# Gate projections of a conformer/attention/MoE layer: seven block products for eight, weight sums made by accumulating loads, the convolution's norm moved into attention slots

## What is computed

```python
proj = x @ w_in[l] + b_in[l]                       # 1024 -> 4608 columns
glu_in, q, k, v, gate_logits = jnp.split(proj, splits, axis=-1)
y_conv = conv_branch(glu_in, ...)                  # a * sigmoid(gate) -> causal depthwise conv, 31 taps
                                                   # -> LayerNorm over 512 channels -> silu -> @ w_conv_out
y_attn = chunked_attention(heads(q), heads(k), heads(v), rel_bias[l]) @ w_attn_out[l]
g_conv, g_attn = jnp.split(jax.nn.sigmoid(gate_logits), 2, axis=-1)     # 2 x 1024 columns
mixed = (g_conv * y_conv + g_attn * y_attn) @ w_o[l] + b_o[l]
x = layer_norm(ALPHA * x + mixed, ln1_g[l], ln1_b[l])
x = layer_norm(ALPHA * x + grouped_moe(x, w_router, b_router, w_gate_up[l], w_down[l]), ln2_g[l], ln2_b[l])
```

## Time and profile before

| what | value |
|---|---|
| median of 3 runs | 1135.43 us (1131.72 to 1138.6) |
| span of the profiled execution | 1130.7 us |
| PE busy | 1098.3 us, 97% |
| DVE busy | 803.2 us, 71% |
| ACT busy | 529.2 us, 47% |
| POOL busy | 227.4 us, 20% |
| chain that ended last | PE 85%, DVE 4%, DMA 4%, ACT 3% |

### The profile page before, as it was taken

How to read it: one execution, slowest core, us unless ns; L and a number is a source line. 1 busy time by engine, 2 the same in 40 slices (tenths; PEclk the granted TensorE clock), 3 DMA queues, 4 the chain that set the end, 5 groups by cost and what they waited for, 6 DMA issues and landing times.

```text
span 1130.7 us, 17012 instructions
## 1 busy us (share of the span) xinstructions
PE 1098.3 (97%) x5583; PEld 913.1 (81%) x5584; DVE 803.2 (71%) x1152; ACT 529.2 (47%) x787; POOL 227.4 (20%) x190
## 2 busy tenths in 40 slices
PE   8999999999999999999999999999999999999984
PEld 7888888888978789878888888787888888888762
DVE  5799999935447766666685588888679556558866
ACT  5111111123456665645331134467578545557755
POOL 0000000000046864757100000013121211212110
PEclk9999999999999999999999999999999999999998
DMA  7121233232111010181632325889999876699966
GB/s 266 56 84 56 83 104 104 83 112 93 57 38 43 19 43 1 65 326 39 251 118 88 142 119 196 278 331 354 324 331 381 311 230 192 236 352 341 368 177 269
DMA packets 49800, 199.58 MB, mean 177 GB/s; under 512 B 7249, under 2 KB 7633, under 8 KB 47682
## 3 DMA queue, kind: packets, MB, share of 16 engines
q1 hardware_dynamic: 43538, 176.19, 41.9%
q0 software_dynamic: 6192, 22.49, 8.0%
HBM read 166.21 MB, written 32.52 MB: 176 GB/s over the span
## 4 chain that ended last, share of the span: by engine, by line
PE 85%; DVE 4%; DMA 4%; ACT 3%; POOL 2%; issue 2%; ACTq 0%; DVEq 0%; SPq 0%; POOLq 0%
PE ps L544 16%; PE ps L546 16%; PE ps L545 16%; PE ps L1570 9%; PE ps L1572 9%; PE ps L1571 9%; PE ps L644 2%; PE ps L630 2%; DMA gu<-in_wexp 2%; PE ps L616 2%; DMA dn_raw<-in_wexp 2%; PE ps L1651 1%; PE ps L1566 1%; POOL pr L499 1%; PE ps L1678 1%
## 5 line engine op out<-in xcount | busy, mean ns | idle before, releaser
L544 PE MATMUL ps<-xh,wh 128*128 128x512 f32 x512 | 203.3, 397 | 2.0 <-DVE xl L1030 1.7
L545 PE MATMUL ps<-xl,wh 128*128 128x512 f32 x512 | 199.5, 390 | 0.0
L546 PE MATMUL ps<-xh,wl 128*128 128x512 f32 x512 | 199.5, 390 | 0.0
L1469 DVE TENSOR_TENSOR gu<-gu (+1 forms) x128 | 148.6, 1220 | 33.6 <-issue 21.5
L499 POOL TENSOR_SCALAR pr<-pr,rinv 128x640 f32<-128x640 f32 (+4 forms) x64 | 95.4, 1503 | 379.7 <-DVE rinv L1153 379.5
L1052 DVE SCALAR_TENSOR_TENSOR cv<-u,dw_t,cv 128x1024 f32<-128x1024 f32 x120 | 154.1, 1284 | 3.7
L1570 PE MATMUL ps<-gu,xgh 128*128 x336 | 134.0, 399 | 4.0 <-DVE gu L1469 2.2
L1463 ACT ACTIVATE gu<-gu (+1 forms) x128 | 124.4, 1048 | 20.6 <-DMA gu<-in_wexp 13.0
L1572 PE MATMUL ps<-gu,xgl 128*128 x336 | 131.9, 393 | 0.0
L1571 PE MATMUL ps<-gu,xgh 128*128 x336 | 131.4, 391 | 0.0
L544 PEld LDWEIGHTS ps<-xh,wh 128*128 128x128 f32 x512 | 96.1, 188 | 25.4 <-issue 6.4
(11 more groups left out here) (278 smaller groups left out, 2022.4 us busy)
## 6 DMA issues: line engine op xcount, KB each, us to landing
gu<-in_wexp SPq DMA_DIRECT2D x64, 1024.0 KB, 9.1
dn_raw<-in_wexp SPq DMA_DIRECT2D x16, 2048.0 KB, 9.8
raw<-in_wblk SPq DMA_DIRECT2D x52, 512.0 KB, 4.2
gate_cols<-gst SPq DMA_DIRECT2D x16, 512.0 KB, 5.3
xf<-acc_rows SPq DMA_DIRECT2D x8, 512.5 KB, 8.1
xraw<-in_xT SPq DMA_DIRECT2D x8, 512.0 KB, 7.3
gcm<-gate_cols SPq DMA_DIRECT2D x8, 512.0 KB, 7.5
gam<-gate_cols SPq DMA_DIRECT2D x8, 512.0 KB, 14.5
```

The lines of the kernel that those rows point to most:

```text
L544: pe.matmul(o, a_h, b_h, start=first, stop=False)
L545: pe.matmul(o, a_h, b_l, start=False, stop=False)
L546: return pe.matmul(o, a_l, b_h, start=False, stop=last)
L1469: eng.tensor_tensor(gu[:, par, k, 1, :], gu[:, par, k, 1, :].bitcast(F32), gu[:, par, k, 0, :], ALU.subtract).then_inc(gu_lo, 1)
```

## The change

A pair of gate blocks (two blocks of 128 columns) against two halves of the inputs and two halves of the tokens is a two-by-two product of blocks. It took eight block products; after the change it takes seven (the Strassen-Winograd scheme), on sums of weight quarters and sums of x quarters, and seven additions of results. A block product is 4 input tiles by 3 matmuls of 512 columns, 12 matmuls. There are 8 pairs (`KC`), so 56 products (`N_UNITS`), in the order 1, 6, 5, 7, 2, 3, 4 (`ORDER`) within a pair.

- **Weights.** A "unit" (`uraw`, `uh`, `ul`, eight slots in the place of the weight ring) is a sum of one to four quarters of 256 KB. The first quarter is loaded, the others are added by DMAs that accumulate into SBUF. All of them, 15 for each pair and 120 in all, are issued by POOL, and each accumulating one waits until the one before it has landed.
- **x.** Four sums of quarters of x are made once by DVE (`input_sums`), split by ACT and DVE (`t_high`, `t_low`).
- **Results.** ACT copies product 1 out of PSUM, DVE makes seven additions of 512 columns for a pair (`gate_sums`), ACT takes the sigmoid in place, SP stores halves of 256 KB.
- **Convolution.** One tap beside each product (`TAPS_A_PRODUCT`), two beside each value tile, the last ten behind the value tiles. The mean comes between the half sums of q and k, the squares behind it, the variance in slot 1 (`VAR_SLOT`), the reciprocal in slots 2 and 3, `normalise` in slots 4 to 7, the silu in slot 9 (`SILU_SLOT`).
- The scaling of the first two biases goes from DVE to POOL. Value tiles use banks 0 to 3, so that the q/k half sums wait for all of them (`v_lo`).

Many semaphores are shared, with new counts; this part of the diff is left out.

```diff
+UNIT_SLOTS = 8
+PARTS = {1: ((0, 0),), 2: ((0, 1),), 4: ((1, 1),), 5: ((1, 0), (1, 1)), 6: ((1, 0), (1, 1), (0, 0)),
+         7: ((0, 0), (1, 0)), 3: ((1, 0), (1, 1), (0, 0), (0, 1))}
+ORDER = (1, 6, 5, 7, 2, 3, 4)
...
+                def add_piece(m, p):
+                    if 0 <= m < N_UNITS and p < len(PARTS[UNITS[m][0]]):
+                        s = m % UNIT_SLOTS
+                        pool.wait_ge(u_in[s], unit_in(m, p - 1))
+                        pool.dma_start(uraw[:, s], unit_rows(m, p), accum_op=ALU.add).then_inc(u_in[s], 16)
+                def load_unit(m):
+                    if m < UNIT_SLOTS:
+                        pool.wait_ge(blk_used, B_V[0] - RING + m // 2 + 1)
+                    elif m < N_UNITS:
+                        pool.wait_ge(blk_used, B_V[0] + m - UNIT_SLOTS + 1)
+                    if m < N_UNITS:
+                        pool.dma_start(uraw[:, m % UNIT_SLOTS], unit_rows(m, 0)).then_inc(u_in[m % UNIT_SLOTS], 16)
+                load_unit(0)
+                for m in range(N_UNITS + 2):
+                    load_unit(m + 1)
+                    add_piece(m, 1)
+                    add_piece(m - 1, 2)
+                    add_piece(m - 2, 3)
...
+                def gate_product(m):
+                    x, q = UNITS[m]
+                    s, bank = m % UNIT_SLOTS, m % 8
+                    pe.wait_ge(u_lo, m + 1)
+                    if m < 8:
+                        pe.wait_ge(u_ready, CB - 1 + (m >= 4))
+                    else:
+                        bank_read(m - 8)
...
+                    for k in range(CB):
+                        last = mm3(ps[:, bank, :], uh[:, s, k], ul[:, s, k], b_h[:, k, :], b_l[:, k, :],
+                                   k == 0, k == CB - 1)
...
-                for g in range(LAST_GATES[0]):
-                    gate_job(g)
-                conv_mean()
-                gate_job(LAST_GATES[0])
-                conv_var()
-                gate_job(LAST_GATES[1])
+                for m in range(N_UNITS):
+                    gate_product(m)
...
+                pe.wait_ge(v_lo, TT)
                 for i in range(2):
                     pe.wait_ge(w_lo, B_Q[0] + i + 1)
...
                     for h in range(2):
                         half_sum(B_Q[0] + i, h, ps[:, 2 * i + h, :], 0, KC).then_inc(qk_done, 1)
+                        if i and h == 0:
+                            conv_mean()
...
+                for m in range(N_UNITS):
+                    if m + 4 < N_UNITS:
+                        unit_low(m + 4)
+                    elif m + 4 < N_UNITS + 2:
+                        low(B_V[0] + m + 4 - N_UNITS)
+                    if m == 0:
+                        glu(CB - 1)
+                    if m:
+                        gate_sums(m - 1)
+                    some_taps(TAPS_A_PRODUCT)
+                gate_sums(N_UNITS - 1)
...
+                def conv_late(n):
+                    if n == 0:
+                        for j in range(1, CB):
+                            square_sum(j)
+                    if n in (2, 3):
+                        dve.wait_ge(sq_done, CB + 1)
+                        for i in range(2 * n - 4, 2 * n - 2):
+                            c = slice(2 * P * i, 2 * P * i + 2 * P)
+                            dve.reciprocal(rstdc[:, c], std[:, c]).then_inc(nrm, 1)
+                    if 4 <= n < 4 + CB:
+                        normalise(n - 4)
```

More of the change, by code:

```diff
@@ L899, in v_high @@
+                for m in range(N_UNITS + 2):
+                    if m < N_UNITS:
+                        copy_product(m)
+                    if m + 4 < N_UNITS:
+                        unit_high(m + 4)
+                    elif m + 4 < N_UNITS + 2:
+                        high(B_V[0] + m + 4 - N_UNITS)
+                    for q, slot in sigmoids_at(m):
+                        gate_sigmoid(q, slot)
                 def v_high(s, t, o):
@@ L952, in _ @@
                 for i in range(2):
-                    act.wait_ge(gs_out[i], 16 * KC)
+                    for slot in range(4):
+                        act.wait_ge(row_moved[4 * i + slot], GATES_STORED)
                 def conv_high(n):
@@ new lines, in _ @@
+                assert taps == CB * CW
+                for i in range(2):
+                    qk_low(i, ps[:, i, :])
+                dve.wait_ge(stat_done, 1)
+                for j in range(CB):
+                    dve.scalar_tensor_tensor(out=cv[:, j, :], in0=psf[:, 4 * HALF:6 * HALF], scalar=-1.0 / DC, in1=cv[:, j, :],
+                                             op0=ALU.mult, op1=ALU.add).then_inc(cent, 1)
+                for i in range(2, 4):
+                    qk_low(i, ps[:, i, :])
@@ L1131, in maxima @@
+                for i in range(2):
+                    for slot in range(4):
+                        dve.wait_ge(row_moved[4 * i + slot], GATES_STORED)
                 def maxima(n):
@@ L2176, in two_a_block @@
         return columns(w).reshape(KC // 2, 2, P, CB, P).transpose(0, 2, 1, 3, 4).reshape(KC // 2, P, KC, P)
[L2177 removed]
+    first, gates = block_columns()
+    w_in = columns(w_in)
+    blocks = np.concatenate([w_in[first], two_a_block(w_conv_out), two_a_block(w_attn_out), columns(w_o), w_in[gates]])
     rel = np.clip(np.arange(P)[:, None] - np.arange(BANDW)[None, :] + 512, -256, 256) + 256
```

434 lines of the change are left out of this document (270 added, 164 removed).

## The result

The changed kernel takes 1205.6 us (median; 1203.5 to 1206.2) against 1134.3 (1131.7 to 1138.6) of the kernel before, run beside it: a ratio of 1.062 with a 95% interval of 1.059 to 1.065. Forecast were 1151, with a range up to 1172. The direction was right; the size, 71 us instead of 15, was not.

What follows compares the result with a forecast made beforehand. PE, busy 97% of the span, was taken to set the time. Late loads (265.2 - 255.7, the break-even), 4.9 in slot 9 and 1.0 for normalising gave 15.4 us more: 1150.8 us against the median 1135.4, range 1126 to 1172.

Steps and rivals of the forecast that it cites:

- the trip L of a first quarter: Gate loads: issue to landing of a unit's first, plain quarter, taken as 3.4 us; upper end 4.7.
- X = 265.2: End of PE's last gate product, at the first value tile: 265.2 us with late loads, 252.4 if they keep up.
- i = 1.0: Gate loads: POOL's time to issue one DMA, 1.0 us, counted five times in a pair's chain.
- M = 4.3: Gate loads: issue to landing of an accumulating quarter, 4.3 us (2.2 to 6.1), counted three times a pair.
- The products: Gates: 56 products of 12 matmuls instead of 768 matmuls, 152.3 us instead of 174.1, 21.8 us less.
- the fourth `u`: Gates, product 4: DVE finishes this convolution input at 110.9 us, PE wants it at 106.1; PE waits 4.9 us.
- Value tiles: Ahead of the q/k half sums: PE waits 3.9 us for all eight value tiles' low halves from DVE.
- Into slot 0: Start of the attention slots: PE waits 2.6 us for the first k and 1.4 for the next pair's weights.
- Slots 0 to 4: Norm's work on DVE: PE waits 2.1 us for the squares, 0.9 in slot 3, 3.2 for q's low half.
- Slot 9: Silu takes 7.2 us on ACT ahead of the exponentials; PE waits 4.9 us.
- the one that the loads keep up: Rival: a pair's loads take under 19.5 us, gates end at 252.4, about 1138 us in all; chance 0.26.
- the high one: Rival: accumulating trips as long as the scatters', from 5.2 us; pair over 24, whole over 1170 us; chance 0.11.

Runs made afterwards that it cites:

- e2: The changed kernel with the later quarters of a unit loaded by plain DMAs that overwrite instead of accumulating: 1163.1 us, first value tile at 260.1 us.
- e7: The changed kernel with first quarters loaded from SP's queue, up to eight units ahead, and only accumulating loads on POOL's: 1182.0 us, ratio 1.043.
- e1: The changed kernel with every unit loaded as one quarter, so no DMA accumulates: 1164.8 us, first value tile at 251.0 us.
- e8: The kernel before with eight waits of 7.2 us, one ahead of every second gate block, each for two chained landings of a zero row: 1210.6 us, ratio 1.069.
- e4: The one-quarter-a-unit kernel (e1) without the norm's work in the attention slots: 1224.6 us with more expert rows; slot 0 to `w_o` 272.4 us against 287.9.
- e6: The changed kernel with POOL's scaling of the two bias tiles moved behind the value tiles: 1197.7 us, ratio 1.057.
- e5: The changed kernel with two quarters in every unit, same 14 loads a pair, never two accumulating in a chain: 1170.1 us (one run), first value tile at 267.3 us.

## Why the prediction was wrong

**The step that failed** is the price of the loads of the units, and in it the trip L of a first quarter: forecast 3.4 us, measured 8.0 where it is in the chain. "X = 265.2" stood on a pair of 21.3 us. What the runs showed:

- *The trips.* The pair is 26.3 us in the rows above, 26.5 in the mean. Term by term: "i = 1.0" is 0.55 between issues, 2.3 us a pair less; "M = 4.3" is 4.7 to 6.0, 2.6 more; "L = 3.4" is 8.0, 4.6 more (6.3 to 8.2 over the pairs). The mechanism, one chain through POOL's queue to the fourth quarter, was the right one, with the waits "before every seventh product" where it put them. I took L from a gather "alone on the queues", while here a first quarter lies behind accumulating ones in a queue. e2 prices the accumulating itself, with what it does to the plain trips, at 45 us of X; e7's edit gives 23. From there X adds up: the first fourth quarter is issued at 105.9 instead of 104.9, seven pairs take 185.7 instead of 149.1, its landing and splits 5.3 instead of 5.8, and the last two products 8.4 instead of 5.4. That is 305.3, and 36.6 of the 40.1 us too few are the pairs'. (A pair has 14 loads, not the "15" of the text; the chain didn't use that number.) By the estimate from the Trainium skill, DMA: Bandwidth & Descriptors, section Anatomy of one DMA, a trip was 2.6 us; e1's plain quarters, with 43% of the DMA engines' time taken, have a median of 2.9, but e2's loads have 3.7, and the accumulating ones 4.8. The measured trips decide.
- *The waits' price.* Named as what would make me wrong, and not priced: "if the granted clock falls in the waits, which no row here lets me price". It does fall. The gates lost 57.8 us against 152.3: 37.7 in ten waits (the 0.9 at X with them) and 20.1 beyond them, 2.5 for each of the eight waits of 3 us and more, near e8's 2.2. But seven of the eight slow stretches lie inside the period that the loads set: at a clock of 1.00 PE would have waited that much longer. Only the last, behind 296.9, moves X, by 2.1 of the 8.4 us for two products. It costs more where DVE and PE wait for one another, behind X.

Point by point, the rest:

- *The products*, "21.8 us less" and "X is 252.4" if the loads keep up: right; 251.0 in e1. The wait for the fourth `u`, 4.9 forecast, is 3.2.
- *Value tiles*, 3.9: 11.4. DVE was held up 4.9 us by POOL's scaling, of which moving it gives back 2.9 ("POOL has some 90 us before anyone needs it: nothing" was right of the deadline and wrong of the price, since DVE stood still meanwhile); the rest is DVE's backlog at X, 6.7 us instead of 0.8. X to slot 0 was put at 53.1; it took 63.6: 7.5 of this wait, and nearly all of the rest is the clock (0.92).
- *Into slot 0*, 2.6 and 1.4: 1.7 and 1.2. *Slots 0 to 4*, 2.1, 0.9 and 3.2: 1.9 for the squares and 3.5 for `ql`. *Slot 9*, 4.9: 4.5. All right within a us. The sum from slot 0 to `w_o`, 13.5 of waits and 1.8 for the moved variance, 15.3, is 18.8 against the kernel before and 15.5 between e4 and e1 (where the 1.4 for the weights is in both, so 13.9 were forecast). What is over goes with the clock: 0.95 in slots 0 to 4, and 0.89 in the 30 us around the silu (426.7 to 456.7).
- *Behind `w_o`* nothing was forecast; it took 3.5 us more, which no run took apart. Nor is it settled why X of e6 lies 5.9 us ahead of the changed kernel's with the same program up to there: it shows how far trips under load can vary between two kernels.

Of the rivals, the one that the loads keep up was refuted by POOL's trips, and the high one came nearest in its numbers (a pair over 24 us, X over 284) but only in part by its reason, "M from 5.2 us": the three accumulating trips of a pair's chain are 5.2 in the mean, which is its lower edge, and the plain quarter's 8.0 does more. The rival that the loads keep up put the whole at 1138; e1, where they do, is 13.8 us behind the kernel before at `w_o`, where that rival had it 2.6 behind, by the wait ahead of the half sums, the slots and the clock.

## What to carry to other kernels

Where PE is at 97%, a wait of several us costs its length and another 2 us at half the clock, while one of 1.1 us costs hardly more than its length. That holds where the wait hangs on PE's own progress, as in e8; there each belongs in the sum at its length plus 2. Where PE waits for a chain with a pace of its own, the period of that chain is the price, and the slow clock is inside it until the last wait. Sums made by accumulating DMAs are first of all a chain of trips (e5), and only then a load on the DMA engines: price the longest chain of one unit by trips under load, against the time from the slot's release to its use, and put plain loads on another queue. An engine with time to spare isn't free to use: ask who stands still while it works. And ask what the change costs where it moves work to: here that was more than the products save, before any load was late (e1).
